# A step of a diffusion backbone on one core: expert programs by token count, loads in another order, gathers by pairs

## The reference

```python
def grouped_moe(h, w_router, b_router, w_gate, w_up, w_down):
    s = sigmoid(t @ w_router)                       # 384 tokens, 16 experts in 4 groups
    # the best group by its two best scores, then the two best experts in it
    gates = ...                                     # two weights per token, their sum 1
    hid = silu(einsum('td,edf->tef', t, w_gate)) * einsum('td,edf->tef', t, w_up)
    hid = hid * gates[:, :, None]
    out = einsum('tef,efd->td', hid, w_down)        # D 1024, hidden 512
x = x + g2 * grouped_moe(h2, ...)
```

## Time and profile before

| | us |
|---|---|
| median of 3 runs | 1332.46 |
| lowest and highest run | 1325.84 and 1333.64 |
| the profiled execution | 1328.36 |
| its span, from the first to the last instruction | 1326.6 |
| PE busy with matmuls | 1087.3 (82%) |
| DVE busy | 410.2 (31%) |
| moved by DMA | 342.83 MB, 258 GB/s over the span |

### The profile page before, as it was taken

The page is one execution under the profiler, slowest core; times in us unless marked ns, Lnnn a source line. Parts: engine busy times, 40 slices in busy tenths (PEclk is TensorE's granted clock), DMA queues, the critical chain, the costliest instruction groups (busy, mean ns, idle before and its releaser), DMA issues.

```text
span 1326.6 us, 12035 instructions
## 1 busy us (share of the span) xinstructions
PE 1087.3 (82%) x4254; PEld 453.4 (34%) x4255; DVE 410.2 (31%) x984; ACT 158.4 (12%) x355; POOL 148.5 (11%) x199
## 2 busy tenths in 40 slices
PE   6999999578867978788784999999687787777891
PEld 1245445242223323333322453555232332223330
DVE  0329877042111101111105488953211111001113
ACT  0211233020000000000003013422000000000001
POOL 0000413111110000000003020040210000000001
PEclk9899999888887989988996999999799988888996
DMA  9933799975769695799998317125286995999825
GB/s 345 384 118 126 231 270 292 244 243 132 298 228 398 227 384 186 269 411 400 389 372 293 124 69 254 64 88 213 67 262 248 370 397 240 369 385 371 330 81 166
DMA packets 80097, 342.83 MB, mean 258 GB/s; under 512 B 7030, under 2 KB 9766, under 8 KB 63630
## 3 DMA queue, kind: packets, MB, share of 16 engines
q1 hardware_dynamic: 56512, 277.89, 55.2%
q0 software_dynamic: 14160, 48.49, 13.4%
q10 hardware_dynamic: 9348, 15.42, 3.5%
HBM read 305.48 MB, written 36.29 MB: 258 GB/s over the span
## 4 chain that ended last, share of the span: by engine, by line
PE 50%; DMA 29%; DVE 9%; issue 6%; POOL 2%; ACT 2%; SPq 1%; POOLq 0%; ACTq 0%; DVEq 0%
DMA ring<-in_w_up_dram 18%; PE ps L1446 14%; PE ps L1159 13%; PE ps L1460 8%; PE ps L1173 5%; DVE scr L888 4%; PE ps L1356 4%; DMA mod_rows<-shiftB 4%; DMA scr<-h_rows,slot_tok 2%; PE ps L1281 1%; DMA ring<-in_w_mod_dram 1%; PE ps L1434 1%; POOL slot_tokens L512 1%; DMA scr<-expert_rows,pick 1%; PE ps L1209 1%
## 5 line engine op out<-in xcount | busy, mean ns | idle before, releaser
L1446 PE MATMUL ps<-ring,scr 128*64 128x512 f32 x1248 | 311.2, 655 | 96.5 <-DMA ring<-in_w_up_dram 86.7
L1446 PEld LDWEIGHTS ps<-ring,scr 128*64 128x64 f32 x1248 | 104.5, 150 | 274.9 <-issue 265.0
L1173 PE MATMUL ps<-ring,cs 128*2 128x512 f32 x384 | 183.5, 629 | 11.9 <-DMA ring<-in_w_mod_dram 11.9
L1460 PE MATMUL ps<-ring,scr 128*64 128x512 f32 x624 | 156.7, 644 | 5.9 <-DVE scr L1131 4.3
L888 DVE SCALAR_TENSOR_TENSOR scr<-scr,convw 128x128 f32<-128x128 f32 (+1 forms) x480 | 160.5, 408 | 0.0
L1159 PE MATMUL ps<-ring,hT 128*128 128x512 f32 (+1 forms) x384 | 146.3, 542 | 0.0
L1118 DVE TENSOR_TENSOR scr<-ps,scr 128x256 f32<-128x256 f32 x32 | 13.6, 424 | 350.1 <-ACT scr L759 350.1
L1356 PE MATMUL ps<-ring,hT 128*128 128x512 f32 x192 | 87.5, 611 | 18.5 <-DVE x L1023 17.1
L1159 PEld LDWEIGHTS ps<-ring,hT 128*128 128x128 f32 x384 | 73.0, 192 | 69.9 <-issue 67.6
L1173 PEld LDWEIGHTS ps<-ring,cs 128*2 128x2 f32 x384 | 31.0, 88 | 145.4 <-issue 139.4
L522 POOL DMA_INDIRECT scr<-h_rows,slot_tok x32 | 29.0, 906 | 455.3 <-PE ps L1434 432.6
(11 more groups left out here) (169 smaller groups left out, 706.0 us busy)
## 6 DMA issues: line engine op xcount, KB each, us to landing
ring<-in_w_gate_dram SPq DMA_DIRECT2D x32, 2048.0 KB, 13.7
ring<-in_w_up_dram SPq DMA_DIRECT2D x32, 2048.0 KB, 19.8
ring<-in_w_down_dram SPq DMA_DIRECT2D x32, 2048.0 KB, 9.5
ring<-in_w_mod_dram SPq DMA_DIRECT2D x23, 2048.0 KB, 15.1
expert_rows<-x POOLq DMA_DIRECT2D x16, 1280.0 KB, 52.8
ring<-in_w_in_dram SPq DMA_DIRECT2D x6, 2048.0 KB, 17.5
expert_rows<-scr ACTq DMA_DIRECT2D x78, 128.0 KB, 7.6
ring<-in_w_out_dram SPq DMA_DIRECT2D x4, 2048.0 KB, 9.0
```

Source lines behind the costliest of these rows:

```text
L1173: mm = pe.matmul(ps[0:2, mod_bank(l, c), :], cs[:, :, k], slot_w(slot_of(n))[:, k, :], start=(k == 0), stop=(k == KD - 1))
L1446: mm = pe.matmul(ps[b * TT:(b + 1) * TT, bank, :].rearrange("p (m n) -> p m n", m=2), src[:, k * TT:(k + 1) * TT], w[:, :, k, b * HF:(b + ...
L1460: mm = pe.matmul(ps[b * TT:(b + 1) * TT, bank, :], src[:, k % 2 * P + k // 2 * TT:k % 2 * P + (k // 2 + 1) * TT], w[:, k, b * SEG:(b + 1) ...
```

## The change

It touches the experts and what prepares them.

1. **Order of loads.** The items of a layer become gate 0, up 0, gate 1, up 1, down 0, and from there gate e, up e, down e - 1. `LEAD` is the item just ahead of the first expert's. In the last layer the last modulation piece is loaded as two halves in two buffers (`split`).
2. **Three programs per expert.** `by_tiles` replaces `overflow`: each engine reads the expert's count and runs `step(1)`, `step(2)` or `step(6)`. In `step(2)` the order on PE is gate_up of e, transposes of the further tile, down of e - 1, gate_up of the further tile, release of gate and up, xT of the next pair, hidden transposes of e, then hidden transposes and down of the further tile. The banks of PSUM are given out anew (`OV` for the further tile).
3. **All 16 experts are written out** on PE, ACT, DVE and (as before) POOL; their loops are gone. SP keeps a loop over pairs.
4. **Gathers by pairs.** One gather fetches 128 rows, 64 of expert 2i and 64 of 2i + 1, with `pair_tok` from two more small matmuls and one copy. `xT` makes eight transposes of 128 rows per pair into two banks; the copies go to `hT`, which is free then.
5. **Compact result rows.** `y_dram` has 16 tiles for the first tiles of the experts and 26 for all further ones (`MORE`). DVE works out where each expert's further tiles begin, by a running sum over the experts, and each token's row, into `pick_y`: some 25 small operations between the place of the tokens and their weights, ahead of `slot_tok`. ACT waits for `rows_ready` in place of `pos_ready`.
6. **The fill** becomes one DMA of 26 tiles, issued by ACT behind its copy of the queries' projection of tile 0.

```diff
-XT, OV_GU, GU, OV_Y, HT, YB = 0, 1, 2, 3, 4, 5
+XT, GU, OV_GU, HT, YB, OV = 0, 2, 3, 4, 5, 7
+MORE = 26
+def gate_item(l, e):
+    return LEAD[l] + (3 * e if e else 1)
+def down_item(l, e):
+    return LEAD[l] + (3 * e + 5 if e < E - 1 else 3 * E)
...
-    y_dram = nc.dram_tensor("expert_rows", (E * CAP, D), F32, kind="Internal").ap()
+    y_dram = nc.dram_tensor("expert_rows", ((E + MORE) * TT, D), F32, kind="Internal").ap()
...
-                with sp.Fori(0, E // 2) as i:
-                    for j in range(2):
-                        for m, w in enumerate((w_gate_v, w_up_v, w_down_v)):
-                            n = EXP_AT[l] + 3 * j + m
-                            s = slot_of(n)
-                            sp.wait_ge(slot_used[s], i + n // SLOTS)
...
+                load_gate_up(0)
+                load_gate_up(1)
+                load_down(0)
+                with sp.Fori(0, E // 2 - 1) as i:
+                    for e in (2, 3):
+                        load_gate_up(e, i)
+                        load_down(e - 1, i)
+                load_down(E - 1)
...
+        def by_tiles(eng, n, step):
+
+            with eng.If(n > TT):
+                with eng.If(n > 2 * TT):
+                    step(NT)
+                with eng.Else():
+                    step(2)
+            with eng.Else():
+                step(1)
...
-                if l == 0:
-
-                    pool.wait_ge(qkT_ready, 4)
-                    for e in range(E):
-                        pool.dma_start(y_dram.rearrange("(e t p) n -> p e t n", t=NT, p=TT)[:, e, 1:NT, :],
-                                       x[0:TT, 0, :].unsqueeze(1).broadcast_to([TT, NT - 1, D])).then_inc(filled_st, 16)
...
+                def gather(i):
+
+                    pool.indirect_dma_start(out=xs[:, i % 2, :], out_offset=None, in_=h2_dram,
+                                            in_offset=bass.IndirectOffsetOnAxis(ap=pair_tok[:, i:i + 1], axis=0))\
+                        .then_inc(gathered[i % 2], 16)
...
+                    if e % 2 and e + 3 < E:
+                        pool.wait_ge(xT_ps, l * (E // 2) + e // 2 + 1)
+                        gather(e // 2 + 2)
...
                 queries(0)
+                if l == 0:
+                    act.dma_start(y_dram[E * TT:, :].rearrange("(r p) n -> p r n", p=TT),
+                                  x[0:TT, 0, :].unsqueeze(1).broadcast_to([TT, MORE, D])).then_inc(filled_st, 16)
                 take_zT(1)
...
+                counts = ps[:, 5, NE:NE + E]
+                step.mark(v.tensor_scalar(row_[:, 0:E], counts, float(2 * TT), float(NT - 2), ALU.is_gt, ALU.mult))
+                step.link(v.tensor_scalar(extra, counts, float(TT), None, ALU.is_gt))
...
+                for n_, far_ in enumerate((1, 2, 4, 8)):
+                    a_, b_ = runs[n_ % 2], runs[1 - n_ % 2]
+                    step.link(v.tensor_tensor(b_[:, E // 2:], a_[:, E // 2:], a_[:, E // 2 - far_:E // 2 + E - far_], ALU.add))
...
+                v.tensor_copy(rows_v[:, :, 1], pmax).then_inc(rows_ready, 1)
...
+                    def step(tiles):
+                        if j == 0:
+                            pe.wait_ge(xsT_ready, l * (E // 2) + i + 1)
+                        if past(g0):
+                            pe.wait_ge(hid_ready, g0)
+                        loaded(gate_item(l, e))
+                        loaded(gate_item(l, e) + 1)
+                        gate_up(GU, e, lambda k: hT[:, i % 2, k, j * TT:(j + 1) * TT]).then_inc(gu_ps, 1)
...
+                        if tiles == 2:
+                            more_transposed()
+                            if e:
+                                down_main(e - 1)
+                            more_gate_up()
+                        for m in range(2):
+                            idle_matmul().then_inc(slot_used[slot_of(gate_item(l, e) + m)], 1)
+                        if j and e + 1 < E:
+                            pe.wait_ge(gathered[(i + 1) % 2], (l * (E // 4) + (i + 1) // 2 + 1) * 16)
+                            xT(i + 1)
+                        if tiles != 2 and e:
+                            down_main(e - 1)
+                        pe.wait_ge(hid_ready, g0 + 1)
+                        hidden_transposes(hid, HT).then_inc(hidT_ps, 1)
+                        if tiles == 2:
+                            more_down()
+
+                    by_tiles(pe, n, step)
...
-                with pe.Fori(1, E // 2 - 1) as i:
-                    expert(i, 0, False, False)
-                    expert(i, 1, False, False)
...
+                for e in range(E):
+                    expert(e)
+                down_main(E - 1)
```

More of the change, by code:

```diff
@@ L219, in build @@
         mid = cut(D)
-        xsT, hid, hidT = mid[:, 0:KD * TT], mid[:, KD * TT:KD * TT + HF], mid[:, KD * TT + HF:D]
+        hid, hidT, ov_hid, ov_hidT = (mid[:, n * HF:(n + 1) * HF] for n in range(4))
         yflat = cut(D)
@@ L1038, in _ @@
                 pmax, psum, wsum, wr_ = (cutr(TILES) for _ in range(4))
+                row_, far = cutr(NE), cutr(NE)
+                runs = [cutr(E // 2 + E) for _ in range(2)]
+                extra, row_base = cutr(E), cutr(E)
+                assert o <= D
                 s_flat = route[:, :, :].rearrange("p t e -> p (t e)")
@@ new lines, in _ @@
+                step.mark(v.tensor_scalar(far, ps[:, 5, 0:NE], float(TT), None, ALU.is_ge))
+                shift = runs[1][:, E // 2:]
+                step.link(v.scalar_tensor_tensor(shift, extra, float(TT), row_base, ALU.mult, ALU.subtract))
+                step.mark(v.tensor_tensor(by_tile(row_), by_tile(ps[:, 5, 0:NE]),
+                                          row_base.unsqueeze(1).broadcast_to([P, TILES, E]), ALU.add))
+                step.link(v.tensor_scalar(shift, shift, float((E - 1) * TT), None, ALU.add))
@@ new lines, in _ @@
+                step.link(v.tensor_tensor(by_tile(far), by_tile(far), shift.unsqueeze(1).broadcast_to([P, TILES, E]),
+                                          ALU.mult))
+                step.link(v.tensor_tensor(row_, row_, far, ALU.add))
+                step.link(v.tensor_tensor(far, row_, lo, ALU.mult))
+                step.link(v.tensor_tensor(row_, row_, hi, ALU.mult))
+                step.mark(v.tensor_reduce(psum, by_tile(far), AX.X, ALU.add))
+                step.link(v.tensor_reduce(pmax, by_tile(row_), AX.X, ALU.add))
@@ L1147, in _ @@
+                    by_tiles(dve, n, step)
+                take_xT(0)
+                for e in range(E):
+                    expert(e)
             for t in range(TILES):
@@ L1414, in _ @@
                 pe.wait_ge(slots_in, (l + 1) * 16)
+                for b in range(2):
+                    pe.matmul(ps[b * TT:(b + 1) * TT, 6, E * NT:E * NT + E // 2], slot_rows_sb[:, :],
+                              ident[0:E * NT, b * NT:E * NT:2 * NT], start=True, stop=True)
                 pe.matmul(ps[0:TT, 6, 0:E * NT], slot_rows_sb[:, :], ident[0:E * NT, 0:E * NT], start=True, stop=True)\
@@ L1469, in down_main @@
                         pe.wait_ge(y_taken, l * E + k - 1)
-                    expert_loaded(i, j, 2)
-                    down(YB + j, j, hidT).then_inc(slot_used[expert_slot(j, 2)], 1)
+                    loaded(down_item(l, k))
+                    down(YB + k % 2, k, hidT).then_inc(slot_used[slot_of(down_item(l, k))], 1)
                 def idle_matmul():
-                    return pe.matmul(ps[0:1, 7, 0:1], ones[:, 0:1], ones[:, 0:1], start=True, stop=True)
-                def expert(i, j, first, last):
-                    e = i * 2 + j
+                    return pe.matmul(ps[0:1, XT, 0:1], ones[:, 0:1], ones[:, 0:1], start=True, stop=True)
@@ L1527, in _ @@
-                expert(E // 2 - 1, 0, False, False)
-                expert(E // 2 - 1, 1, False, True)
-                down_main(E - 1, E // 2 - 1, 1)
+                for e in range(E):
+                    expert(e)
+                down_main(E - 1)
 _INS = ['x_prompt', 'x_sample', 'cache_k', 'cache_v', 'c', 'c_ctx', 'w_mod', 'b_mod', 'norm1_g', 'norm2_g', 'w_in',
```

315 lines of the change are left out of this document (173 added, 142 removed).

## The result

After: 1343.72 us (median of 8 runs, 1339.27 to 1349.5); before, beside it: 1332.63 (1325.84 to 1336.28). The ratio is 1.0091 [1.0059, 1.0123]: 0.9% slower, where 8% faster was forecast. The profiled execution took 1349.12 us, its span is 1347.3.

What follows compares the result with a forecast made beforehand. Experts were taken to wait for weights, partly because nobody had asked for the next load. Gains of 47 (layer 0), 36 (layer 1) and 21.5 us (fill), 104.5 in all, took 1328.4 to 1224 us; range 1188 to 1265.

Steps and rivals of the forecast that it cites:

- Three unrolled programs: Head of each expert on PE: a jump over about 930 instructions costs 1.9 us an expert, bounds 0 and 3.4.
- 1.4 us each: PE's nine one-tile first passes before the change lose 12.4 us together, mid-program breaks included: 1.4 us each.
- 1.9 us an expert: Price taken per expert on PE for the jump, with slower matmuls after such a gap.
- the upper bound of 3.4: Per expert on PE: jump and mid-program break each time, at about the longest seen, 3.4 us.
- the third rival: Expert heads: code fetches queue behind weights; phases' gain gone at about 5.2 us an expert, fill's at 5.8; chance 0.04.
- the 4 that the prediction named as a sign of being wrong: Before gate_up on PE: idle by issue over 4 us an expert would show the forecast wrong.
- The sum: Expert phases: PE alone 271 and 288 us, with waits 282 and 298; gains 47 and 36, plus 21.5 for the fill.
- The smaller fill: Attention to scatter in layer 0: 21 MB become 6.8 MB on ACT's queue, gain 21.5 us.
- Gathers by pairs: Ahead of the experts: expert 2's wait goes, transposes save 0.6 us an expert; a 128-row gather lands in 6.1 us.
- Row arithmetic on DVE: Before slot_tok: some 25 small operations, 5 us a layer, hidden behind a wait of 9.54 us.
- Order of loads: Expert weights asked for earlier: DMA hole shrinks to about 0 after one two-tile expert, 3 to 11 us after two.

Runs made afterwards that it cites:

- experiment 3: The changed kernel without the program for three or more tiles, on every engine, the choice still at the head of the expert: 1228.60 us, 0.9249.
- experiment 6: The changed kernel with one loop body for PE's five further tiles and the choice of program behind the first gate_up: 1218.85 us, 0.9138.
- experiment 5: The changed kernel with PE's five further tiles as one loop body instead of five copies, the choice still at the head: 1298.92 us, 0.9765.
- experiment 2: The changed kernel with no choice on PE, this input's seven two-tile experts written out; other engines choose as before: 1226.18 us, 0.9210.
- experiment 7: The kernel before, with only its PE loop over pairs of experts written out: 1385.44 us, 1.0373.
- experiment 12: The changed kernel with loop body and late choice, the second pair's gather moved back to its old place: 1221.87 us, 0.9177.
- experiment 8: The changed kernel without the program for three or more tiles, with the old order of loads: 1251.63 us, 0.9345.
- experiments 1: The changed kernel with PE's waits and first gate_up of every expert ahead of the choice of program: 1266.38 us, 0.9528.

## Why the prediction was wrong

**The step that failed** is "Three unrolled programs": "1.4 us each", "1.9 us an expert" with slower matmuls. The 1.4 us of the earlier trace rows were read as the price of a jump. They were what was left of it behind a gate_up in flight; the jump itself stood in the trace among the sequencer's own instructions, 5.8 us long. With the move to the head of the expert the cover went: the gap is 3.0 to 4.9 us there late in layer 0, and gate_up after it takes 8.5 to 8.8 us and not 7.09, about 5.5 us together. That lies above the upper bound of 3.4, and at the third rival's break-even, 5.2 to 5.8, as is the time. That rival had the mechanism (fetches at every head, a resident loop lost) with a chance of 0.04; its cause, the queue behind weights, is 1.3 us of 6.2. Idle by issue before gate_up, 148.1 us, is 4.6 us an expert, over the 4 that the prediction named as a sign of being wrong. The prediction knew that loop passes showed no gap, and did not ask what a gap would be where nothing runs.

The Trainium skill, "Runtime: NRT & Kernel Launch", section "Instruction fetch mechanics", says that a taken branch whose target isn't in the current window of two pages waits for the fetch of the target's page. The traces agree: the jumps of 5.4 to 7.3 us end behind such a transfer. The same section of the Trainium skill has instructions come in blocks of 16 KiB, 256 instructions, so that two pages, if a page is such a block, are 512 instructions, an estimate. The traces agree with the block (16,384 bytes a packet), and the estimate fits the code that runs once: the jumps over some 230 instructions were mostly short (experiment 3), over some 340 short or long (experiment 6), over some 470 (experiment 5) and 930 (after) all long. It does not fit the loop of before, whose jumps over some 590 took 0.21 us. That the Trainium skill's section prefers full unrolling where possible fits experiment 2's straight line, and not code where branches remain: experiment 7 lost 3.7%.

**The sum.** PE alone was forecast at 271 and 288 us a layer, 282 and 298 with waits. Where jumps are short or covered (experiment 6), the phases take 270.8 and 286.6, the time 1218.85 beside 1224. That is near in part by luck. Of the parts, visible stalls were smaller than forecast (some 25 us for 61 in both layers) and waits for weights larger (34 us for 21); the phases together came out 23 us shorter than 282 and 298, and the stretch between them took 292.5 us where before took 278.1, a loss of 14 that the sum didn't have.

**The smaller fill** was right: 21.5 us forecast, 22.9 measured in that stretch, and ACT's ten small loads take 0.26 to 0.62 us each. Its issue on ACT took 0.71 us. Of the three runs on the fill, the large one on POOL's queue agrees with the price; the small one on that queue and the large one on ACT's, 40 us earlier, would each have done.

**Gathers by pairs** took the wait away, as said, though a gather of 128 rows landed in 12.9 us (median) and not in the 6.1 of the forecast; in experiment 12 the early gather is worth some 3 us in layer 0, which the total cannot show.

**Row arithmetic on DVE** was hidden but for about 1 us: the first gather comes 27.35 us after the first scatter, 26.45 before.

**Order of loads.** The wait for up weights is gone from the chain, and SP's wait for the down matmuls (L1570, L1460 before) is 66.3 us for 539.5, but most of it has moved to the release of gate and up. The hole in the transfers at a further tile is not gone: in expert 7 of layer 0 the DMA share (the last number but one) is 0.01 for 12 us.

```profile
SPq L392 <- PE ps L1584: 472.8, 28, 35.8
SPq L400 <- PE ps L1570: 66.3, 21, 3.7
...
514.00:526.00 12.00, 12.00 (x62) 4.95 (x60) 1.45 (x3) 0.97 (x2) 0.00 (x0) 1.00 0.01 2
```

PE is busy throughout those 12 us, and the chain has no load of the experts' weights: with a stall of 5.5 us an expert, PE and not the loads sets the pace. What the order is worth without stalls is in experiment 8.

**Open.** A jump's price is not its distance alone: L386 of before, over some 470 instructions, took 0.2 us three times in layer 0 and 3.3 to 3.6 in layer 1, experiment 5's 6.1, and experiment 6's over some 340 anything from 0.3 to 7.0. The traces show what the rest depends on: in the kernels of experiments 1, 3 and 5 to 7 and in before, all 29 branches on PE of 0.9 to 3.8 us end 1.3 to 1.6 us behind a packet of q8 that started before the jump or within 1.4 us of its start, so its block was on the way or asked for soon. When the sequencer asks for a block ahead of time was not tried.

## What to carry to other kernels

A gap behind a queue in flight is a remainder, not a price: read the duration of the sequencer's own instruction before moving it. Put a data-dependent choice behind the longest queued work that all its outcomes share, keep rare programs short (a loop body) so that the common one is near, and do not unroll a loop whose branches are cheap only because its code is there. Before a large transfer, look what small writes stand behind it on its own queue while it lasts.

## What the runs showed of the hardware

In after, a taken jump on PE took 5.4 to 7.3 us, and each had the transfer of a block of 16,384 bytes of instructions inside it, 1.3 to 1.6 us ahead of its end. Over some 230 instructions most took 0.2 to 0.4 us (experiment 3), and 0.21 in the loop of before, which needed no such transfer for 220 us. DVE's and ACT's branches for the same programs took 0.04 to 0.07 us. After a gap of 3.85 us the granted clock was 0.57 from 592.5 to 596.5 and 1.00 from 596.5 to 601 (a part at 1.2 GHz, then 2.4 throughout): 4.0 x 0.43 = 1.7 us of work lost, as much as that gate_up took longer (8.78 for 7.09).
